# Squares added and constants converted on GpSimd at the start of a two-layer decoder trunk; lambdas through TensorE

## The reference

```python
for l in range(DEPTH):
    h = h + 0.5 * _swiglu(_rmsnorm(h, ffn1_norm[l]), ffn1_w1[l], ffn1_w3[l], ffn1_w2[l])
    u = _rmsnorm(h, mix_norm[l])
    z = u @ w_in[l]
    ...
    lam_init = 0.8 - 0.6 * math.exp(-0.3 * l)
    o_a = _diff_attention(a_q, a_k, a_v, diff_lq1[l], diff_lk1[l], diff_lq2[l],
                          diff_lk2[l], diff_subln[l], lam_init)
    ...
    h = h + m @ w_out[l]
    h = h + 0.5 * _swiglu(_rmsnorm(h, ffn2_norm[l]), ffn2_w1[l], ffn2_w3[l], ffn2_w2[l])
return _rmsnorm(h, final_norm)
```

```python
lam = (jnp.exp(jnp.sum(lq1 * lk1)) - jnp.exp(jnp.sum(lq2 * lk2)) + lam_init)
```

## Time and profile before

| | |
|---|---|
| median of 3 runs | 2503.44 us (2503.03 to 2506.02) |
| the profiled execution | 2503.49 us, span 2501.7 us |
| busy: TensorE, DVE, ScalarE, GpSimd | 2478.0, 2133.8, 1526.9, 4.4 us |
| DMA | 235.88 MB, 94 GB/s on average |

### The profile page before, as it was taken

How to read it: one execution, slowest core, us unless ns; L and a number is a source line. 1 busy time by engine, 2 the same in 40 slices (tenths; PEclk the granted TensorE clock), 3 DMA queues, 4 the chain that set the end, 5 groups by cost and what they waited for, 6 DMA issues and landing times.

```text
span 2501.7 us, 50059 instructions
## 1 busy us (share of the span) xinstructions
PE 2478.0 (99%) x15824; PEld 2248.1 (90%) x15824; DVE 2133.8 (85%) x3881; ACT 1526.9 (61%) x3061; POOL 4.4 (0%) x13
## 2 busy tenths in 40 slices
PE   8999999999999999999999999999999999999998
PEld 7999888888889989998889998888888898899987
DVE  8999868888888779998789997788888986799986
ACT  7666447777764456664466654578777554566643
POOL 0000000000000000000000000000000000000000
PEclk9999999999999999999999999999999999999999
DMA  4322321211123222223322223221111322223332
GB/s 157 110 108 101 110 102 60 68 60 60 66 91 106 93 102 101 101 101 118 111 94 101 101 96 128 82 68 60 68 60 60 111 93 101 94 101 110 108 110 102
DMA packets 65272, 235.88 MB, mean 94 GB/s; under 512 B 7232, under 2 KB 7488, under 8 KB 65088
## 3 DMA queue, kind: packets, MB, share of 16 engines
q1 hardware_dynamic: 65088, 233.64, 26.7%
HBM read 231.51 MB, written 2.10 MB: 93 GB/s over the span
## 4 chain that ended last, share of the span: by engine, by line
PE 91%; DVE 5%; issue 2%; ACT 1%; DMA 1%; DVEq 0%; SPq 0%; ACTq 0%
PE ps L665 28%; PE ps L666 28%; PE ps L667 28%; PE ps L906 2%; PE ps L837 1%; DVE w_lo L1782 1%; PE ps L826 1%; PE ps L880 1%; PE ps L879 1%; PE ps L828 1%; DVE area L1782 1%; PE ps L893 0%; PE ps L843 0%; PE ps L895 0%; DMA h<-x 0%
## 5 line engine op out<-in xcount | busy, mean ns | idle before, releaser
L1136 ACT ACTIVATE w_hi<-w_raw 128x512 fp32r<-128x512 f32 (+1 forms) x876 | 627.9, 723 | 474.4 <-PE ps L667 216.0
L1782 DVE TENSOR_TENSOR w_lo<-w_raw,w_hi 128x512 fp32r<-128x512 f32 (+1 forms) x876 | 703.1, 809 | 111.8 <-ACT w_hi L1136 96.0
L665 PE MATMUL ps<-u_hi,w_hi 128*128 128x256 f32 (+1 forms) x2432 | 787.7, 324 | 5.9 <-DVE w_lo L1782 3.2
L667 PE MATMUL ps<-u_hi,w_lo 128*128 128x256 f32 (+1 forms) x2432 | 780.8, 321 | 0.0
L666 PE MATMUL ps<-u_lo,w_hi 128*128 128x256 f32 (+1 forms) x2432 | 780.5, 321 | 0.0
L666 PE MATMUL ps<-area,w_hi 128*128 128x256 f32 (+1 forms) x1764 | 580.8, 329 | 0.0
L665 PEld LDWEIGHTS ps<-u_hi,w_hi 128*128 128x128 f32 x2432 | 463.3, 190 | 41.8 <-DVE w_lo L1782 4.5
L667 PEld LDWEIGHTS ps<-u_hi,w_lo 128*128 128x128 f32 x2432 | 463.2, 190 | 34.8
L666 PEld LDWEIGHTS ps<-u_lo,w_hi 128*128 128x128 f32 x2432 | 463.4, 191 | 32.6 <-issue 1.4
L665 PE MATMUL ps<-area,w_hi 128*128 128x256 f32 (+1 forms) x1400 | 480.0, 343 | 0.4 <-DVE h L1804 0.4
L667 PE MATMUL ps<-area,w_lo 128*128 128x256 f32 (+1 forms) x1400 | 477.6, 341 | 0.0
(11 more groups left out here) (188 smaller groups left out, 2915.1 us busy)
## 6 DMA issues: line engine op xcount, KB each, us to landing
w_raw<-weights SPq DMA_DIRECT2D x435, 512.0 KB, 3.6
h<-x SPq DMA_DIRECT2D x4, 512.0 KB, 8.3
out<-scratch_whole SPq DMA_DIRECT2D x8, 256.0 KB, 2.5
scratch_whole<-const_b SPq DMA_DIRECT2D x1, 512.0 KB, 10.2
scratch_whole<-const_r SPq DMA_DIRECT2D x1, 320.0 KB, 8.9
scratch_whole<-lambdas SPq DMA_DIRECT2D x1, 256.0 KB, 2.5
cst<-const SPq DMA_DIRECT2D x1, 137.0 KB, 7.9
par<-params SPq DMA_DIRECT2D x1, 94.0 KB, 2.6
```

The lines of the kernel that those rows point to most:

```text
L665: pe.matmul(dst, hi, x_hi, start=start, stop=False, **kw)
L667: return pe.matmul(dst, lo, x_hi, start=False, stop=stop, **kw)
L1136: return act.activation(dst, src, ACT.Copy)
L1782: return dve.tensor_tensor(dst, src, hi_part.bitcast(F32), ALU.subtract)
```

## The change

Four things are done to the beginning, and the FFN's head changes with them.

- The lambda vectors come as eight columns of params (64 partitions). Their own DMA goes. DVE multiplies four columns by four, TensorE sums over the partitions with a matrix of ones that GpSimd sets (`lam_ones`), behind the fifth idle product, and ScalarE's Exp reads that sum in PSUM. Idle products are 15, not 18.
- The seven adds of the first squares move from DVE to GpSimd. DVE's `split(2)` stands directly behind `split(1)`.
- GpSimd also converts the four blocks of constants, after the adds. DVE waits for them before `plain_gate(0)`.
- ScalarE makes the four `scaled` of a layer's first FFN before that FFN: for layer 0 ahead of the squares, for layer 1 at the end of the loop's body, which is run in the last round too. The first FFN then begins with the LN_EXP table load, and `norm` has none there.
- In every FFN's head ScalarE makes the hi part of `split(1, raw=0)` before the first silu, and DVE its lo part before `plain_up(0)`.

```diff
-P_END = P_WF + DEPTH * ND * N_FOX
+P_LAM = P_WF + DEPTH * ND * N_FOX
+P_END = P_LAM + 4 * DEPTH
...
-IDLE_PRODUCTS = 18
+IDLE_PRODUCTS = 15
...
+        lam_ones = area_whole[:, SEQ:SEQ + P]
...
-            sp.dma_start(scratch[:, 5 * SEQ:6 * SEQ], lambdas).then_inc(lam_landed, 16)
             sp.dma_start(par[:], params).then_inc(par_landed, 16)
...
             pool.memset(area[:, 0:SEQ].bitcast(F32), 0.0).then_inc(warm_set, 1)
+            pool.memset(lam_ones, 1.0).then_inc(warm_set, 1)
+
+            for d in range(1, ND):
+                pool.wait_ge(sq_set, d)
+                pool.wait_ge(acc_set, d)
+                pool.tensor_tensor(acc, acc, first_square(d), ALU.add).then_inc(acc_set, 1)
+            pool.wait_ge(small_landed, 16 * 2)
+            pool.tensor_copy(cst_b[:], scratch[:, 0:IN_BF16 * P])
+            pool.tensor_copy(cst_r[:], scratch[:, IN_BF16 * P:ROUNDED * P])
+            pool.tensor_copy(base_l[:], scratch[:, 1024:1024 + SEQ])
+            pool.tensor_copy(base_r[:], scratch[:, 1024 + SEQ:1024 + 2 * SEQ]).then_inc(const_set, 1)
...
-            for _n in range(IDLE_PRODUCTS):
+            for n in range(IDLE_PRODUCTS):
                 pe.matmul(ps[:, 7, :], area[:, 0:P], area[:, 0:SEQ], start=True, stop=True)
+                if n == 4:
+
+                    pe.wait_ge(warm_set, 2)
+                    pe.wait_ge(lam_in, 1)
+                    pe.matmul(ps[:, 6, 0:2 * DEPTH], lam_ones, lam[:, 8:8 + 2 * DEPTH], start=True, stop=True
+                              ).then_inc(lam_mm, 1)
...
-            def norm():
-
-                act.preload_act_table_set(LN_EXP)
+            def norm(table=True):
+
+                if table:
+                    act.preload_act_table_set(LN_EXP)
...
+            def scaled_four(own):
+
+                for k in range(4):
+                    scaled(k, own + k)
...
-            def ffn(gain):
-                own = gain - ND
-                scaled(0, own)
-                scaled(1, own + 1)
-                scaled(2, own + 2)
-                scaled(3, own + 3)
+            def ffn(gain, first):
+                if first:
+                    act.preload_act_table_set(LN_EXP)
+                else:
+                    scaled_four(gain - ND)
...
-                norm()
+                norm(table=not first)
                 act.preload_act_table(ACT.Silu)
                 all_sum_hi(0)
+                split(1, raw=0)
                 silu(plain_tile(0))
-                split(1, raw=0)
...
-            act.wait_ge(lam_in, 1)
-            act.activation(lam[:, 4:8], lam[:, 8:12], ACT.Exp).then_inc(lam_out, 1)
+            act.wait_ge(lam_mm, 1)
+            act.activation(lam[:, 4:8], ps[:, 6, 0:2 * DEPTH], ACT.Exp).then_inc(lam_out, 1)
...
             split(1, after=0)
+            scaled_four(P_GAIN)
             act.activation(acc, h[:, 0:SEQ], ACT.Square).then_inc(acc_set, 1)
...
-            act.wait_ge(small_landed, 16 * 2)
-            hi(cst_b[:], scratch[:, 0:IN_BF16 * P])
-            hi(cst_r[:], scratch[:, IN_BF16 * P:ROUNDED * P])
-            hi(base_l[:], scratch[:, 1024:1024 + SEQ])
-            hi(base_r[:], scratch[:, 1024 + SEQ:1024 + 2 * SEQ]).then_inc(const_set, 1)
             with c.turns(0, DEPTH) as layer:
-                ffn(layer * (3 * ND) + (P_GAIN + ND))
+                ffn(layer * (3 * ND) + (P_GAIN + ND), True)
                 mixer(layer, layer * (3 * ND) + (P_GAIN + 2 * ND))
-                ffn(layer * (3 * ND) + (P_GAIN + 3 * ND))
+                ffn(layer * (3 * ND) + (P_GAIN + 3 * ND), False)
+
+                scaled_four(layer * (3 * ND) + (P_GAIN + 3 * ND))
             norm()
...
                 dve.wait_ge(rstd_set, c.next(rstd_set))
+
+                dve.wait_ge(const_set, 1)
                 plain_gate(0)
                 sum_lo(token_sum(ALL, 0), LAST, 0)
+                split(1, raw=0)
                 plain_up(0)
-                split(1, raw=0)
...
-            pairs = tile(4)[:, 0:n * HEAD]
-            dve.tensor_tensor(pairs, SQ[:, 0:n * HEAD], SQ[:, n * HEAD:2 * n * HEAD], ALU.mult).then_inc(vec_done, 1)
-            dve.wait_ge(vec_done, c.next(vec_done))
-            dve.reduce_sum(lam[:, 8:8 + n], pairs.rearrange("p (a b) -> p a b", b=HEAD), AX_X).then_inc(lam_in, 1)
+            dve.wait_ge(par_landed, 16)
+            n = 2 * DEPTH
+            dve.tensor_tensor(lam[:, 8:8 + n], par[:, P_LAM:P_LAM + n], par[:, P_LAM + n:P_LAM + 2 * n], ALU.mult
+                              ).then_inc(lam_in, 1)
             dve.wait_ge(lam_out, 1)
...
             split(1)
-            dve.wait_ge(acc_set, c.next(acc_set))
-            for d in range(1, ND):
-                add_square(first_square(d))
-                if d == 4:
-                    split(2)
+            split(2)
```

More of the change, by code:

```diff
@@ L176, in turns, with trunk @@
         self.read()
-def trunk(nc, x, stream, params, lambdas, const, const_r, const_b, out):
+def trunk(nc, x, stream, params, const, const_r, const_b, out):
     ctx = ExitStack()
@@ L445, in trunk @@
         warm_set = sem("warm_set")
-        lam_landed = sem("lam_landed")
         par_landed = sem("par_landed")
@@ L472, in trunk @@
         lam_in = sem("lam_in")
+        lam_mm = sem("lam_mm")
         lam_out = sem("lam_out")
@@ L2701, in _ @@
             c.skip(tail_read, 9)
-            dve.wait_ge(lam_landed, 16)
-            n = DEPTH * 2
-            pairs = tile(4)[:, 0:n * HEAD]
-            dve.tensor_tensor(pairs, SQ[:, 0:n * HEAD], SQ[:, n * HEAD:2 * n * HEAD], ALU.mult).then_inc(vec_done, 1)
-            dve.wait_ge(vec_done, c.next(vec_done))
-            dve.reduce_sum(lam[:, 8:8 + n], pairs.rearrange("p (a b) -> p a b", b=HEAD), AX_X).then_inc(lam_in, 1)
+            dve.wait_ge(par_landed, 16)
+            n = 2 * DEPTH
+            dve.tensor_tensor(lam[:, 8:8 + n], par[:, P_LAM:P_LAM + n], par[:, P_LAM + n:P_LAM + 2 * n], ALU.mult
+                              ).then_inc(lam_in, 1)
             dve.wait_ge(lam_out, 1)
-            dve.wait_ge(par_landed, 16)
             for layer in range(DEPTH):
@@ L2734, in _ @@
             split(1)
-            dve.wait_ge(acc_set, c.next(acc_set))
-            for d in range(1, ND):
-                add_square(first_square(d))
-                if d == 4:
-                    split(2)
+            split(2)
+            c.skip(acc_set, ND)
+            c.skip(sq_set, ND - 1)
             with c.turns(0, DEPTH) as layer:
@@ L2839, in small_params @@
         p[:, P_WF + n * ND * N_FOX:P_WF + (n + 1) * ND * N_FOX] = wf.reshape(P, -1)
+    rows = [a[f"diff_l{x}{m}"][n] for x in "qk" for n in range(DEPTH) for m in (1, 2)]
+    p[:HEAD, P_LAM:P_END] = np.stack(rows, 1)
     gains.append(a["final_norm"])
@@ L2842, in small_params @@
     return p
-def lambda_rows(a):
-    rows = [a[f"diff_l{x}{m}"][n] for x in "qk" for n in range(DEPTH) for m in (1, 2)]
-    return np.tile(np.concatenate(rows)[None, :], (P, 1))
 def kernel(**inputs):
@@ L2860 @@
         "params": small_params(a),
-        "lambdas": lambda_rows(a),
         "const": c, "const_r": r, "const_b": b,
```

## The result

| | before | changed |
|---|---|---|
| median | 2504.01 us (2501.95 to 2506.93, 20 runs) | 2508.07 us (2506.58 to 2509.99, 20 runs) |
| span of the profiled execution | 2501.7 us | 2506.2 us |
| unit 1, ones-product, unit 4 start | 17.09, 23.19, 38.42 | 14.95, 26.78, 41.15 |
| from the last ones-product to the end | 11.7 us | 12.7 us |

The ratio of the changed kernel to the one before is 1.0014, with a 95% interval of 1.0008 to 1.0020: some 3.5 us slower, within the 0.2% but clear of noise. 2505.0 was forecast, in a range up to 2510.0, with 0.80 for "within 0.2%". The sign and the two places were right; the size was forecast too small, and the first of the rivals, the fall of the clock, makes up most of the difference.

A forecast was written before the change was run, and what follows sets the result against it. TensorE, busy for 99% of the span, was taken to bound the kernel. +0.50 us at unit 4's start and +1.05 at the end gave +1.55 on 2503.49: 2505.0 us, range 2500.9 to 2510.0.

The forecast's parts named there:

- the two places: Where time was forecast to be lost: the start, up to unit 4, +0.50 us; the end, +1.05 us.
- the first of the rivals, the fall of the clock: TensorE drops to 1.2 GHz after the long stall before unit 2, losing 2.9 us: 2507.9; chance 0.28.
- The first loads: Kernel's start: without lambdas' DMA, x and everything up to w_lo of `split(1)` come 0.55 us earlier.
- Lambdas' steps at nothing: Kernel's start: lambdas' ScalarE and DVE steps fall into a 3.0 us wait for x and cost nothing.
- GpSimd's add: First squares: seven dependent adds, 1.30 us each from 17.95, let the ones-product start at 27.05.
- X: Start of TensorE's unit 4, forecast at 38.92 against 38.42: +0.50 us.
- The mutual wait: Rival: GpSimd's adds and DVE's two-input operations wait for each other in turn; unit 4 +6.3, end 2510.8; chance 0.15.
- The end: Last round: four unread scalings delay table load and rstd, so DVE's output products start later: +1.05 us.
- Conversions and the second memset at nothing: Kernel's start: GpSimd's four conversions and its second memset finish before they are needed and cost nothing.
- Units 3 and 4 without waits: First FFN: the stalls before units 3 and 4 go; one long stall before unit 2 replaces them.
- The order in the later heads at nothing: Later FFNs' heads: silu and `split(1)` in the other order cost nothing, covered by full TensorE.
- The seam at nothing: Between the layers: unit 0 of layer 1 waits for u_lo, hole 2.45 us, untouched by the change: no cost.

The follow-up runs named there:

- e1: Kernel before with only the lambda part: lambdas in params, summed by TensorE, 15 idle products; unit 4 at 36.03, span 2500.8 us.
- e11: Same kernel as e1, run again and timed against the kernel before; ratio 0.9996 (0.9987 to 1.0006).
- e5: Changed kernel with 24 idle products ahead of each ones-product in the FFNs; unit 4 at 38.82, 11.89 us behind the ones-product.
- e4: Changed kernel with the LN_EXP table loaded earlier in the FFN's end, none behind the last scalings; last ones-product to end 11.7 us.
- e8: e6 plus seven GpSimd adds that nobody reads beside DVE's adds; DVE's adds 1.70 us apart, ones-product at 27.88.
- e3: Changed kernel with the ones-product behind unit 2 instead of ahead of it; unit 4 at 39.2.
- e6: Changed kernel with the adds of squares back on DVE and the four scalings back at the FFN's head; median 2501.40 us, ratio to before 0.9985.
- e9: e6 with the four conversions back on ScalarE behind the squares; median 2500.24 us, ratio to before 0.9983.
- e12: e9 with split(1, raw=0) again behind the first silu and first up in every FFN's head; unit 4 at 35.94.
- e7: e6 with eight of the fifteen idle products moved into the loop ahead of unit 0; median 2503.41 us.
- e10: e6 with GpSimd's conversions held until DVE's last add; median 2500.34 us, ratio to before 0.9982.

## Why the prediction was right in sign and too small in size

*The first loads* (taken 0.55, between 0.46 and 0.9): wrong. x lands 1.7 to 2.6 us earlier, ScalarE starts on it 1.8 earlier and unit 1 comes 2.1 earlier (e1, e11). The bounds were too narrow: they priced a slot and the bytes of one DMA, and x gained more than the two together, for a reason that stays open.

*Lambdas' steps at nothing, since they fall into the wait for x*: wrong. With x at 5.0 the wait has ended before they have, and Exp at 5.82 and DVE's steps until 7.13 hold u_hi and u_lo back. Some 0.9 us (5.89 less 5.0) is lost by that at u_hi; what of it reaches unit 4 no run shows, for all kernels with the new lambdas have the same order there.

*GpSimd's add* (1.30 from start to start, 27.05 for the ones-product): 1.41 to 1.44, and one of 2.2. With the chain's start at 16.15 instead of 17.95 that gave 26.78; two misses that cancel, which is luck. So is in part the 1.30 itself: it adds a row of GpSimd's to one of DVE's, and no run shows that an add is made up so.

*X* (38.92): 41.15. The step that failed is "then 0.97 + 2 x 5.45": it held products at 0.23 us through a hole of 5 us, which is the forecast's choice against its own rival. The clock fell, and e5 prices it at 2.5 us (2.9 in the rival; 1.8 in e4). The argument against it, that no hole of the trace had brought a fall, was weak: the longest was half as long, and the one at the seam (2.45) brought none in that one profile, while ten of the fourteen show a fall there.

*The mutual wait* (0.15): its mechanism is real (e8), its price in the changed kernel was not what was said. One add was lengthened by 0.8 us; DVE's loss of 5.8 us in across and second (5.72 + 3.41 less twice 1.67, the conversions' share included) lay under TensorE's own wait, as e3 shows by laying it bare.

*The end* (+1.05): +1.0, with the cause as said (e4). *Conversions and the second memset at nothing*: right in the changed kernel, where TensorE's long wait covers what the conversions cost DVE; in e6 they cost 0.97 us. *Units 3 and 4 without waits*: right. *The order in the later heads at nothing*: right; from unit 4 to the last product ahead of the seam the two kernels differ by 0.1 us. In the first head the order is worth nothing in the changed kernel by its rows (w_lo is ready at 38.4, TensorE comes to unit 4 at 41.15), but 1.45 us in e9 (e12). *The seam at nothing*: 0.4 us longer in this profile; the early scalings may have part in it, which stays open.

## What to carry to other kernels

Work moved to an idle engine joins the path if another engine waits for its result in order: price the whole chain of dependent instructions there and what stands queued behind the wait, before counting what the first engine gains. An engine "with nothing to do" isn't free either if its work lengthens that of the busy one, as GpSimd's did DVE's here, and a hole that it opens in TensorE can be charged again behind the hole in clock. Small steps that fall into a wait have to be priced anew when the change shortens that wait. Here the small part of the change, one DMA less ahead of x and w_lo ahead of silu and up, was the gain, and the part that moved the most work was the loss.

## What had not been expected of the hardware

The clock falls after short holes too, and not every time. Of fourteen profiles the seam's hole of 2.1 to 3.1 us was followed by products 0.43 us apart in ten (e1 to e7, e10 to e12) and by products 0.23 apart in four (before, changed, e8, e9). Busy time by stage at the seam, e6 and then e9 (columns as in the earlier trace rows):

```profile
1249.20:1252.40 3.20, 3.16 (x8) 2.49 (x9) 2.96 (x4) 1.25 (x2) 0.00 (x0) 0.50 0.04 13
```
```profile
1248.70:1252.00 3.30, 3.30 (x15) 2.72 (x16) 3.06 (x4) 1.57 (x2) 0.00 (x0) 1.00 0.05 12
```

e1 was 2.52 us ahead of the kernel before at the seam and 0.96 ahead 3.5 us later, so a fall costs 1.56 us. A difference of that size between two spans says nothing until the seam has been looked at; it is a third of what this change did.

GpSimd's conversions, which read one input, lengthen DVE's operations too: beside e10's, three of the four across of 128x256 are 0.67 to 0.83 us long instead of 0.48.
